# Low weight parts written over the raw weights: six slots of two buffers for four of three, and the rounds one unit further behind

## The reference

```python
for layer in range(DEPTH):
    h = _rmsnorm(x, norm_mix[layer])
    if layer % 2 == 0:
        x = x + _mlstm_retention_mixer(h, positions, l0_w_in, ..., l0_w_out)
    else:
        x = x + _gated_deltanet_mixer(h, l1_w_in, ..., l1_w_out)
    h = _rmsnorm(x, norm_ffn[layer])
    x = x + (jax.nn.silu(h @ w_gate) * (h @ w_up)) @ w_down
return _rmsnorm(x, final_norm)
```

## Time and profile before

| | us |
|---|---|
| median of 3 runs (2753.36 to 2754.13) | 2753.4 |
| the profiled execution, its own time | 2752.32 |
| its span, first to last instruction | 2750.5 |
| PE busy | 2720.7 |
| DVE busy | 1743.8 |
| ACT busy | 1418.8 |
| 16 DMA engines, mean rate | 186 GB/s |

### The profile page before, as it was taken

The page is one execution under the profiler, slowest core; times in us unless marked ns, Lnnn a source line. Parts: engine busy times, 40 slices in busy tenths (PEclk is TensorE's granted clock), DMA queues, the critical chain, the costliest instruction groups (busy, mean ns, idle before and its releaser), DMA issues.

```text
span 2750.5 us, 37187 instructions
## 1 busy us (share of the span) xinstructions
PE 2720.7 (99%) x13334; PEld 2264.6 (82%) x13334; DVE 1743.8 (63%) x2387; ACT 1418.8 (52%) x2005; POOL 87.1 (3%) x79
## 2 busy tenths in 40 slices
PE   9999999999999999999999999999999999999998
PEld 7888888888888888888888887887888888888886
DVE  5544665666666665558686868656656666666444
ACT  5444555444444444458787877644454444444443
POOL 0000000000000000001111111000000000000000
PEclk9999999999999999999999999999999999999999
DMA  8564466666666666656555656555666666666664
GB/s 258 154 187 151 153 192 186 196 191 192 194 194 191 193 192 196 192 179 190 156 183 155 183 160 194 174 178 176 197 192 192 193 195 191 192 195 192 208 194 150
DMA packets 263888, 510.94 MB, mean 186 GB/s; under 512 B 20416, under 2 KB 20672, under 8 KB 263504
## 3 DMA queue, kind: packets, MB, share of 16 engines
q1 hardware_dynamic: 259792, 494.54, 59.8%
q0 software_dynamic: 3152, 11.57, 1.4%
q10 hardware_dynamic: 816, 3.15, 0.3%
HBM read 503.91 MB, written 5.28 MB: 185 GB/s over the span
## 4 chain that ended last, share of the span: by engine, by line
PE 93%; DVE 3%; ACT 2%; issue 1%; DMA 1%; DVEq 0%; SPq 0%; ACTq 0%
PE acc L589 29%; PE acc L595 29%; PE acc L590 29%; PE aux L806 2%; DVE wlo L1475 1%; PE aux L642 1%; PE aux L812 1%; DVE arena L1900 0%; PE aux L792 0%; PE aux L800 0%; DVE arena L1941 0%; DMA wraw<-in_l_w_in 0%; DVE arena L1938 0%; ACT whi L1001 0%; DVE arena L1917 0%
## 5 line engine op out<-in xcount | busy, mean ns | idle before, releaser
L1475 DVE TENSOR_TENSOR wlo<-wraw,whi 128x1024 fp32r<-128x1024 f32 x928 | 1142.3, 1239 | 780.1 <-ACT whi L1001 777.9
L1001 ACT ACTIVATE whi<-wraw 128x1024 fp32r<-128x1024 f32 x928 | 978.1, 1059 | 1102.1 <-PE acc L595 1041.8
L589 PE MATMUL acc<-whi,hT_hi 128*128 128x512 f32 x2624 | 1034.5, 394 | 0.5 <-ACT arena L1011 0.5
L590 PE MATMUL acc<-whi,hT_lo 128*128 128x512 f32 x2624 | 1023.4, 390 | 0.0
L595 PE MATMUL acc<-wlo,hT_hi 128*128 128x512 f32 x2624 | 703.5, 390 | 6.0 <-DVE wlo L1475 6.0
L595 PEld LDWEIGHTS acc<-wlo,hT_hi 128*128 128x128 f32 x2624 | 491.9, 188 | 112.7 <-DVE wlo L1475 10.6
L589 PEld LDWEIGHTS acc<-whi,hT_hi 128*128 128x128 f32 x2624 | 493.9, 188 | 102.0 <-ACT arena L1011 0.8
L590 PEld LDWEIGHTS acc<-whi,hT_lo 128*128 128x128 f32 x2624 | 493.9, 188 | 99.9
L589 PE MATMUL acc<-whi,arena 128*128 128x512 f32 x1088 | 423.7, 389 | 3.2 <-ACT whi L1001 3.2
L590 PE MATMUL acc<-whi,arena 128*128 128x512 f32 x1088 | 423.3, 389 | 0.0
L595 PE MATMUL acc<-wlo,arena 128*128 128x512 f32 x1088 | 290.8, 389 | 0.0
(11 more groups left out here) (257 smaller groups left out, 1165.2 us busy)
## 6 DMA issues: line engine op xcount, KB each, us to landing
wraw<-in_l_w_in SPq DMA_DIRECT2D x304, 512.0 KB, 4.2
wraw<-in_l_w_gate SPq DMA_DIRECT2D x176, 512.0 KB, 3.7
wraw<-in_l_w_up SPq DMA_DIRECT2D x176, 512.0 KB, 3.7
wraw<-in_l_w_down SPq DMA_DIRECT2D x176, 512.0 KB, 4.3
wraw<-in_l_w_out SPq DMA_DIRECT2D x96, 512.0 KB, 4.5
arena<-decay_sums POOLq DMA_DIRECT2D x16, 512.0 KB, 5.1
o_rounds<-arena POOLq DMA_DIRECT2D x3, 1024.0 KB, 5.3
arena<-o_rounds ACTq DMA_DIRECT2D x3, 1024.0 KB, 5.4
```

Of the source, the lines that this page charges most:

```text
L589: nc.tensor.matmul(pair[m], hi[:, k, tok], wh, start=first, stop=False)
L590: nc.tensor.matmul(pair[m], lo[:, k, tok], wh, start=False, stop=False)
L1001: nc.scalar.activation(whi[:, s, :], wraw[:, s, :], ACT.Copy).then_inc(hi_done, 1)
L1475: V.tensor_tensor(wlo[:, s, :], wraw[:, s, :], whi[:, s, :].bitcast(F32), ALU.subtract).then_inc(lo_done, 1)
```

## The change

The low part is written over the raw weights: wlo is a second name (in the format fp32r) for the memory of wraw. The same 48 KB a partition then hold six slots of two buffers. Since wraw is only free when PE has read the low part, SP's wait before a load of unit u becomes unit_used >= u - 5; the first six units are loaded without a wait. ACT and DVE wait for unit_used >= u - 5 likewise. On ACT and DVE the rounds of phase l1 stand behind unit w + 3's part (ROUND_AHEAD = 3); all else that went by AHEAD stays at two. Since six does not divide the units of a phase's body, the slot is now computed from the unit's number in the whole kernel; the loops of the phases out and dn and of l0a become straight code, and those of gu run over three pairs of blocks at a time (each_pair: the pairs 0 and 1 in straight code, then three turns of three).

```diff
-SLOTS = 4
+SLOTS = 6
+PAIRS = 3
@@
+ROUND_AHEAD = 3
@@
+        wraw_at = nc.sbuf_base
         wraw = sb("wraw", [P, SLOTS, 2 * NB])
+        wlo = nc.alloc_sbuf_tensor_at("wlo", [P, SLOTS, 2 * NB], F32R, offset=wraw_at)
         whi = sb("whi", [P, SLOTS, 2 * NB], F32R)
-        wlo = sb("wlo", [P, SLOTS, 2 * NB], F32R)
@@
+        slot_of = lambda name, w: (UNIT0[name] + w) % SLOTS
+
+        def each_pair(eng, name, first, run):
+
+            for i in range(first, 2):
+                run(i, i)
+            if name in ("gu0", "gu1"):
+                with eng.Fori(0, (FF // NB - 2) // PAIRS) as q:
+                    for c in range(PAIRS):
+                        run(q * PAIRS + (2 + c), 2 + c)
@@ SP
-                sp.wait_ge(lo_done, u - (SLOTS - 1))
-                sp.dma_start(wraw[:, j % SLOTS, :].rearrange("p (k n) -> p k n", k=2),
-                             col_block(w, col)[:, 2 * j:2 * j + 2, :]).then_inc(raw_in[j % SLOTS], 16)
+                if u >= SLOTS:
+                    sp.wait_ge(unit_used, u - (SLOTS - 1))
+                sp.dma_start(wraw[:, u % SLOTS, :].rearrange("p (k n) -> p k n", k=2),
+                             col_block(w, col)[:, 2 * j:2 * j + 2, :]).then_inc(raw_in[u % SLOTS], 16)
@@ PE, gemm_block
-                    slot = (slot0 + j) % SLOTS
+                    slot = slot_of(name, i0 + w0 + j)
@@ PE, ffn
-                with pe.Fori(1, FF // NB) as i:
-                    body(name, i, 2, hT_hi, hT_lo, [None, None])
+                each_pair(pe, name, 1, lambda i, i0: body(name, i, 2, hT_hi, hT_lo, [None, None], i0))
@@ ACT, body
-                        s = w % SLOTS
-                        act.wait_ge(raw_in[s], i * (n_body * upb // SLOTS * 16) + 16 * ((UNIT0[name] + w) // SLOTS + 1))
+                        s = slot_of(name, i0 * n_body * upb + w)
+                        act.wait_ge(raw_in[s], (i - i0) * n_body * upb * 16 // SLOTS + 16 * ((UNIT0[name] + i0 * n_body * upb + w) // SLOTS + 1))
@@ ACT and DVE, hook_l1
-                rounds(gdn, w - AHEAD)
+                rounds(gdn, w - ROUND_AHEAD)
```

More of the change, by code:

```diff
@@ L429, in phase, with run @@
                 upb = UPB[name]
-                with sp.Fori(lo, hi) as i:
+                def run(i, i0):
                     for b, (wt, col) in enumerate(cols(i)):
@@ L433, in phase @@
                             u = UNIT0[name] + (i * n_body + b) * upb + j
-                            sp.wait_ge(lo_done, u - (SLOTS - 1))
-                            s = (b * upb + j) % SLOTS
+                            sp.wait_ge(unit_used, u - (SLOTS - 1))
+                            s = slot_of(name, (i0 * n_body + b) * upb + j)
                             sp.dma_start(wraw[:, s, :].rearrange("p (k n) -> p k n", k=2),
                                          col_block(wt, col)[:, tiles[2 * j]:tiles[2 * j] + 2, :]).then_inc(raw_in[s], 16)
+                if hi == FF // NB:
+                    each_pair(sp, name, lo, run)
+                else:
+                    for i in range(lo, hi):
+                        run(i, i)
             def gate_columns(w, col, layer):
@@ L596, in lo_products, with gemm_block @@
                 return mm
-            def gemm_block(name, base_u, base_b, hi, lo, slot0, parity, midway=None, fresh=False, between=None, tiles=range(64)):
+            def gemm_block(name, base_u, base_b, hi, lo, w0, parity, i0, midway=None, fresh=False, between=None, tiles=range(64)):
                 upb = UPB[name]
@@ L615, in gemm_block @@
                     if between is not None:
-                        between(slot0 + j)
+                        between(w0 + j)
             def gate_products(layer):
@@ L644, in transposes, with body @@
                 return mm
-            def body(name, i, n_body, hi, lo, midways, fresh=(), between=None, tiles=range(64)):
+            def body(name, i, n_body, hi, lo, midways, i0, fresh=(), between=None, tiles=range(64)):
                 for b in range(n_body):
@@ L664, in xt @@
                     return f if name == "out0" else None
-                body(name, 0, 2, hi, lo, [None, xt(0, 1)], between=between, tiles=tiles)
-                with pe.Fori(1, 2) as i:
-                    body(name, i, 2, hi, lo, [xt(i, 0), xt(i, 1)], tiles=tiles)
+                body(name, 0, 2, hi, lo, [None, xt(0, 1)], 0, between=between, tiles=tiles)
+                body(name, 1, 2, hi, lo, [xt(1, 0), xt(1, 1)], 1, tiles=tiles)
                 if name != "dn1":
@@ L681, in ffn @@
             def ffn(name, after, n0):
-                body(name, 0, 2, hT_hi, hT_lo, [None, None], between=last_x_block(after))
-                with pe.Fori(1, FF // NB) as i:
-                    body(name, i, 2, hT_hi, hT_lo, [None, None])
+                body(name, 0, 2, hT_hi, hT_lo, [None, None], 0, between=last_x_block(after))
+                each_pair(pe, name, 1, lambda i, i0: body(name, i, 2, hT_hi, hT_lo, [None, None], i0))
                 return lambda w: pe.wait_ge(flo_done, n0 + FF // NB) if w == FKT // 2 - 3 else None
@@ L975, in between_l1 @@
                     o_transposes(O_SLOTS.index(w))
-            body("l1", 0, 24, hT_hi, hT_lo, [None] * 24, between=between_l1)
+            body("l1", 0, 24, hT_hi, hT_lo, [None] * 24, 0, between=between_l1)
             def last_round(w):
@@ L1062, in residual_phase @@
                 body(name, 0, 2, hook)
-                with act.Fori(1, 2) as i:
-                    body(name, i, 2, hook)
+                body(name, 1, 2, hook, 1)
             def last_x_block(name):
@@ L1091, in ffn @@
                 body(name, 0, 2, hook)
-                with act.Fori(1, FF // NB) as i:
-                    body(name, i, 2, hook)
+                each_pair(act, name, 1, lambda i, i0: body(name, i, 2, hook, i0))
                 return lambda j: f_hi(FF // NB) if j == 12 else None
@@ L1552, in residual_phase @@
                 body(name, 0, 2, hook)
-                with dve.Fori(1, 2) as i:
-                    body(name, i, 2, hook)
+                body(name, 1, 2, hook, 1)
                 def last_x_block(j):
@@ L1610, in ffn @@
                 body(name, 0, 2, hook)
-                body(name, 1, 2, hook)
-                with dve.Fori(2, FF // NB) as i:
-                    body(name, i, 2, hook)
+                each_pair(dve, name, 1, lambda i, i0: body(name, i, 2, hook, i0))
                 def last_f(j):
@@ L1844, in _ @@
             mixer = l0_mixer()
-            body("l0a", 1, 2, lambda i, b, j: next(mixer) if b == 0 and j == 1 else None)
+            body("l0a", 1, 2, lambda i, b, j: next(mixer) if b == 0 and j == 1 else None, 1)
             body("l0b", 0, 2, lambda i, b, j: l0_slots(mixer, b * UPB["l0b"] + j - AHEAD))
```

18 lines of the change are left out of this document (9 added, 9 removed).

## The result

The changed kernel takes 2759.3 us (median of 18 runs, 2755.6 to 2763.2), the kernel before 2753.4 (2751.6 to 2755.0): ratio 1.0022, 95% interval 1.0015 to 1.0029. It is 6 us slower, where 11 us less were forecast, and outside the range. Its profiled execution took 2756.1 us.

The account below looks back on a forecast made before the run. PE, busy 2720.7 of 2750.5 us, was taken as the bound, so only its stalls and clock dips could be won. 7.5 + 1.7 + 1.0 + 1.7 - 0.8 = 11.1 us off 2753.4 gave 2742.3 us, range 2739.5 to 2749.5.

Parts of the forecast that it names:

- The conv(Q) behind it is helped by the same amount: Layer 1's rounds: the convolution of Q gains the same lead, one unit of 2.72 us, as the low parts.
- The 7.5 us: Layer 1's rounds: gain from the steps one unit further back, 8.2 us less 0.7 still short in round 3.
- What is late next: Rounds' steps whose results PE reads: conv(V0) is closest, with a margin of 1.9 us that stays.
- the 8.2 us: Layer 1's rounds: PE's loss to late low parts, 7.3 us in eight stalls plus 0.9 in longer low-product groups.
- The chain starts at the same time: Layer 1's rounds: VectorE's chain of 11 leaf steps starts when it did, with one low part more in hand.
- 0.3 us to spare: Round 0: low part there by 1308.35, wanted at 1308.63, so no stall.
- The dip at 1709: Round 3: half-clock stretch after the 2.02 us stall at 1708.11 goes, 1.7 us gained.
- Layer 0: Layer 0's projections: earlier load starts the gate chain 1.0 us sooner; the half-clock stretch after it goes, 1.7 us.
- Part 2 in steady parts, in place, start, loops: Six slots with loads released by PE, low part over its input, kernel start, straightened loops: 0 us each.
- The stall at out1: Stall at 1867 for o_split(3), 3.2 us: stays, and a half-clock stretch may now follow, half of 1.7, -0.8 us.
- Rival A: Layer 1's rounds: late loads start the leaf chain 1.6 us later, 5.6 us lost, 2748 us; chance 0.16.
- Rival C: Layer 1's rounds: transfers over 7.1 us make twelve handovers late, 19 us lost, slower at 2762 us; chance 0.08.

Follow-up runs that it names:

- e4: Changed kernel with level_t before token_major(Q) in TensorE's step 25: 2749.9 us, ratio 0.9988 to the kernel before.
- e5: Changed kernel with level_t before token_major(Q) on TensorE and ScalarE's round step ahead of the block copies: 2746.1 us, ratio 0.9975 to the kernel before.
- e6: Changed kernel's six slots of two buffers, but rounds two units behind, and level_t before token_major(Q): 2750.3 us, ratio 0.9990 to the kernel before.
- e8: Kernel before with only level_t moved before token_major(Q) in TensorE's step 25: 2752.9 us, ratio 1.000 to the kernel before.
- e3: Changed kernel with ScalarE's round step ahead of the copies out of the accumulator (qkv_out, z_out): 2753.9 us, ratio 1.0005 to the kernel before.
- e1: Changed kernel with ROUND_AHEAD 2 instead of 3 (six slots, old distance): 2749.98 us, ratio 0.9989 to the kernel before.

## Why the prediction was wrong, step by step

- **"The conv(Q) behind it is helped by the same amount"**: this is the step that failed in rounds 0 and 3. The lead of one unit goes to the low parts alone; the convolution is itself one of the rounds' steps, and with "as many high and low parts as before" in front of it, it comes no earlier (41.3 to 41.5 us behind the first leaf step in round 0). The 7.5 us were the low parts' stalls taken as the whole loss. They were one symptom of VectorE's backlog; without them TensorE met its end a step later, at token_major(Q). What is late next was asked of conv(V0) alone. By the estimate above some 5 of the 8.2 us could not be won; 2.2 us of waits for low parts and 7.4 at token_major stand in place of the 6.0. That TensorE waits there for VectorE's backlog is shown by e4 and e5 (the waits shrink when TensorE is given other work there) and by e6 and e8 (no gain where the low parts still wait).
- **"The chain starts at the same time"** failed in rounds 1 and 2, by 2.3 and 3.3 us, and by 0.9 in round 0. By the same estimate this alone makes the waits at token_major(Q) in rounds 1 and 2, and it is why the "0.3 us to spare" of round 0 became a stall of 0.9. "Between two steps lie as many high and low parts" was true, and looked at parts only: the copies of finished blocks changed sides (e3: 5.4 us), and the high part ahead of the step is one whose load comes later (0.9 us in round 0, and in round 1, where 1.0 of the 2.3 comes with the slots alone, e1).
- **The dip at 1709 (1.7)**: one came back 7 us later and a longer one arose in round 2. The forecast said a dip may follow stalls over 2 us and then did not count with new stalls.
- **Layer 0 (1.0 + 1.7)**: right. The stall fell from 2.37 to 1.36 us in starts, the dip went; e1 shows it alone with 3 us. The dip near 163 stands in all three traces with four slots and in none of the nine with six.
- **Part 2 in steady parts, in place, start, loops (0)**: right. The low part's median is 1.225 us (1.226 before), the loads' 3.7 (3.9 before), and TensorE's steady pace is unchanged.
- **The stall at out1 (-0.8 for a dip)**: the stall stayed at 3.4 us in starts, and the changed kernel's trace has no dip there, so the term cost nothing in it. But it was sized too small: a dip follows in eight of eleven traces and costs 1.6 us, or 2.8 in e5.
- **Rival A** had one of the causes of a later chain. In round 0 the load that it named took 5.9 us beside the decay rows (between its 3.9 and 6.8) and the chain was 0.9 later, within its -1.3 to +1.6, where the forecast took 0; in rounds 1 and 2 the same came of loads beside the store. It priced this with the low parts' gain still in hand: 2748. **Rival C** had the sign and named the line that would show it (TensorE waiting at L792, now L810), but by transfers of 7.1 us and more: none in the rounds took over 6.6. That its time, 2762, is near the measured one is luck. A rival with the floor at silu(Q) and with the copies was missing.

Left open: how much the late loads cost by themselves. To move the 1 MB store away from them wasn't tried: ScalarE's leaf set-up waits for it. e3's round 1, 2.2 us later than before, bounds it there from above. Why one stall of 2 us is followed by a dip and another isn't is open too.

## What to carry to other kernels

When a stall comes from an engine's backlog, removing it helps only up to the next thing that reads the same backlog: follow that engine's work to the point where its queue is empty, and ask who waits there. A queued step that is moved changes its order against everything in that queue that stays, so list the fixed neighbours (copies, table loads, waits on others) and not only the work it moves with. And when a chain goes to and fro between two engines, price the move of each: here VectorE's alone cost 29 us, ScalarE's alone 11, and both together 9, against the old distance with the same slots.

## What the runs showed of the hardware that was not expected

Stretches at 1.2 GHz can cost more here than the stalls that precede them. A stall of 2.2 us in round 2 brought 6.8 us at half clock (3.3 us lost). The stall at out1's start, 3.4 us in eleven traces, was followed by no dip in three, by 3.4 us at half clock in seven and by 6.8 in e5. Stalls of 2.2 us in round 0 (the changed kernel and e3) were followed by none, one of 1.3 in round 3 of the changed kernel by 3.4 us. The runs of a kernel spread by as much: the eight timed runs of e5 lie within 1.5 us, the changed kernel's 18 within 7.6; that dips make this spread fits the granted clocks (0.998 in the short spans, 0.995 in the longest) and was not tested by itself.

A 512 KB load beside a 1 MB store of another queue took 6.6 us instead of 3.7, and that store 7.2. A low part written over its own input took as long as one written elsewhere (median 1.225 and 1.226 us).
